# Sample keys turned by VectorE in blocks, latent queries in four column groups, expansions moved between the samples

## The chip, the cores and the metric

The kernel runs on one core of a Trainium2 chip. The metric is the device time of one execution in microseconds. The kernel before took 1524.16 us (median of 3 runs, 1523.92 to 1525.11).

## What is computed

One inference step of a two-layer trunk for a prompt of 512 tokens and for 8 samples of one token each. Layer 0 is a gated token MLP and a ConvFFN, layer 1 latent attention and a ConvFFN; everything is float32. The change touches the attention of layer 1 alone. There each sample attends over 2048 cached positions plus its own new one. A cached position has a latent of 256 numbers (`ckv`) and a rotary key of 64 (`kr`); both are shared by the 8 heads:

```python
s = (einsum('nthc,nsc->nhts', ql, ckv) + einsum('nthr,nsr->nhts', qp, kr)) * ATTN_SCALE
p = softmax(where(k_pos <= pq, s, -inf))
out = einsum('nhts,nsc->nthc', p, ckv)        # then o = out @ w_uv per head, and @ w_o
```

The query side `ql` is the head's query times `w_uk`. The prompt attends causally over its own 512 latents. The cache is paged: sample n's rows are gathered by a page table.

## The kernel before, in words

All activations lie transposed: features on the 128 partitions, 520 columns (512 prompt tokens, 8 samples). Each engine has its program written out by hand, in a fixed order, and the engines meet at semaphores. The weights of the dense layers stream through `ws`, are split into a high and a low part (`split`, L1559), and are multiplied in three products (L602).

The changed part stands between the query projections (L913) and prompt attention (L1107). In order:

- GpSimd gathers a sample's keys (L560 to L572): 128 partitions, each with 16 consecutive cache rows, as `lat` [16, 256] and `lar` [16, 64]. Three buffers (`RING`); the gather of sample g waits from g = 3 on for the weighted sum of sample g - 3 (`pv_done`).
- `turn(s, f)` (L945) transposes the keys on TensorE, ten fills of four 128x128 blocks each, into four PSUM banks. ScalarE and VectorE copy the fills into `kt` in turn (`turned_block`, L1447 and L1871).
- L998 to L1016: latent queries of the samples (`ukt` x `qn`), a pick of the rotary queries, copies into `qz` (per chunk 32 columns, of which 8 heads are used), and the samples' scores over their own new row.
- `score(s)` (L966): 12 matmuls of 512 columns with 32-column weights, four column groups, each holding one quarter of the positions.
- VectorE takes the maximum of each row of the scores (L1907) and its negative (L1909); ScalarE takes the exponentials (L1460); `turn_exps` (L978) transposes them in four 128x128 blocks, VectorE copies them (L1918), `weigh` (L985) makes the weighted sum of the latents (16 matmuls of 256 columns), ScalarE copies it out (L1468).
- The loop L1018 runs sample s's scores, then the transposes of sample s + 1 around `turn_exps(s)`, then `weigh(s)`.
- After the loop `expand(g)` (L1035) makes the prompt's keys and values: 16 expansions of two matmuls with 512 columns. Between them stand the small matmuls that merge the four quarters and the own row of each sample (L1057, L1062, L1063, L1071, L1080), with a chain of small VectorE operations (L1930 to L1990). Then `new_rows` (L1084) transposes the new cache rows, which ScalarE copies (L1488) and GpSimd writes out (L573). Prompt attention starts when `os_ready`, `n_ready` and the last copies are there (L1102).
- SyncE loads the weights `w_o` once all scores are done (L478), since `kt` lies over `ws`.

Of the kernel before, what the change touches and what calls it, by code (L numbers as in the profile page):

```python
# [39 lines left out]
FILLS = 10  # L40
# [35 lines left out]
CONST_COLS = K_SUB + 2  # L76
# [30 lines left out]
def constants():  # L107
# [21 lines left out]
    c[:, K_SELT:K_SELT + P] = p[:, None] == p[None, :] % 32  # L129
# [41 lines left out]
def trunk(nc, a, outs):  # L171
    ctx = ExitStack()
    with ctx:
# [13 lines left out]
        def plan(base, *items):  # L187
# [30 lines left out]
        selt = cst[0:H, K_SELT:K_SELT + P]  # L218

# [36 lines left out]
            ("osb", [NS, CL], F32), ("cksn", [320], F32), ("small", [16], F32), ("ml", [2 * NS], F32), ("st4", [GRP, 2 * NS], F32),  # L256
            ("gst", [GRP, 2, NS], F32), ("wd", [GRP + 1, NS], F32), ("wdl", [GRP, NS], F32), ("lsum", [3, NS], F32),
# [5 lines left out]
        kt, qz, kt_end = plan(ws_base, ("kt", [FILLS, 512], F32), ("qz", [4, NS, 32], F32))  # L263
        assert kt_end <= ws_base + 2 * size([STAGES, 1024])
        pe_, pts, pt_end = plan(tmp_base, ("pe_", [2, 512], F32), ("pts", [2, 512], F32))
# [4 lines left out]
        v, o, _ = plan(arena, ("v", [4, D], F32), ("o", [H, T], F32))  # L270
        ppt1, kn, ppt0, pr_end = plan(
            arena + size([4, D]) + size([H, T]), ("ppt1", [4, SEQ], F32), ("kn", [H, SEQ], F32), ("ppt0", [4, SEQ], F32))
        assert pr_end <= proj_end
        ppt = [ppt0, ppt1]
        pp, okn, ownp, olT, ok_end = plan(
            tmp_base, ("pp", [LAG, SEQ], F32), ("okn", [2, 320], F32), ("ownp", [KC, NS, H], F32), ("olT", [KC, H, NS], F32))
        assert ok_end <= arena
# [6 lines left out]
        def S(name):  # L284
# [35 lines left out]
        ukT_done, ukt_ready, ql_done, qsel_done, qz_clear, qz_ready, so_done, so_ready, sn_done, sn_ready, zpad = (S(n) for n in (  # L320
            "ukT_done", "ukt_ready", "ql_done", "qsel_done", "qz_clear", "qz_ready", "so_done", "so_ready", "sn_done", "sn_ready", "zpad"))
        kv_done, kv_read_a, kv_read_v, nT_done, n_ready, n_sent = (S(n) for n in (
            "kv_done", "kv_read_a", "kv_read_v", "nT_done", "n_ready", "n_sent"))
        cT_done, kt_a, kt_v, sc_done = (S(n) for n in ("cT_done", "kt_a", "kt_v", "sc_done"))
        mx_done, neg_ready, e_done, gat_done, merge, wd_exp, sct_done = (S(n) for n in (
            "mx_done", "neg_ready", "e_done", "gat_done", "merge", "wd_exp", "sct_done"))
# [32 lines left out]
        def st(k, g):  # L359

            return small[:, LAG * k + g % LAG:LAG * k + g % LAG + 1]

# [33 lines left out]
        def _(sp):  # L396
# [81 lines left out]
            sp.wait_ge(sc_done, NS)  # L478
# [114 lines left out]
        def _(pe):  # L593
# [351 lines left out]
            def turn(s, f):  # L945

                m = FILLS * s + f
                if f == 0:
                    pe.wait_ge(d_lat[s % RING], 32 * (s // RING + 1))
                if m < 4:  # L950
                    pe.wait_ge(ukt_ready, m + 1)
                elif m % 2:
                    pe.wait_ge(kt_v, (m - 4) // 2 + 1)
                else:
                    pe.wait_ge(kt_a, (m - 4) // 2 + 1)
                for i in range(4):
                    if f < 8:
                        j, c = f % GRP, f // GRP
                        src = lat[s % RING][:, 8 * (j // 2) + 2 * i + j % 2, c * P:(c + 1) * P]
                    else:  # L960
                        k = 8 * (f - 8) + 2 * i
                        src = lar[s % RING][:, k:k + 2, :].rearrange("p i c -> p (i c)")
                    mm = pe.transpose(psum[:, 4 + m % 4, i * P:(i + 1) * P], src, ident)  # L963
                mm.then_inc(cT_done, 1)

            def score(s):  # L966

                pe.wait_ge(kt_a, 5 * (s + 1))
                pe.wait_ge(kt_v, 5 * (s + 1))
                wait(pe, e_done, s - 1)  # L970
                for b in range(3):
                    for j in range(GRP):
                        q = qz[:, b if b < 2 else 2 + j % 2, s, :]
                        keys = kt[:, 4 * b + j, :] if b < 2 else kt[:, 8 + j // 2, :]
                        mm = pe.matmul(psum[32 * j:32 * j + 32, s % 2, :], q, keys, start=(b == 0), stop=(b == 2))  # L975
                mm.then_inc(sc_done, 1)

            def turn_exps(s):  # L978
                pe.wait_ge(e_done, s + 1)
                wait(pe, pts_ready, s)  # L980
                for i in range(4):
                    mm = pe.transpose(psum[:, 2, i * P:(i + 1) * P], pe_[:, s % 2, i * P:(i + 1) * P], ident)
                mm.then_inc(pT_done, 1)

            def weigh(s):  # L985
                pe.wait_ge(pts_ready, s + 1)
                wait(pe, osn_ready, s)
                for i in range(4):
                    for j in range(GRP):
                        mm = pe.matmul(psum[32 * j:32 * j + 32, 3, 0:CL], pts[:, s % 2, i * P + 32 * j:i * P + 32 * j + 32],  # L990
                                       lat[s % RING][:, 8 * (j // 2) + 2 * i + j % 2, :], start=(i == 0), stop=(i == 3))
# [61 lines left out]
            for g in range(4):  # L1053
                expand(g)
# [998 lines left out]
```

## Time and profile before

| | us |
|---|---|
| median of the runs | 1524.16 |
| the profiled execution | 1521.48 |
| its span, first to last instruction | 1519.2 |
| TensorE matmuls busy | 1466.4 (97%) |
| VectorE busy | 886.2 (58%) |
| ScalarE busy | 548.0 (36%) |
| GpSimd busy | 174.3 (11%) |
| mean granted clock of TensorE | 0.976 |

Engines in the profile: PE is TensorE's matmuls, PEld its weight loads, DVE VectorE, ACT ScalarE, POOL GpSimd, SP SyncE. A row of the chain of work that ended last gives start, length and what; a row of the lines gives line, engine, operation, output <- input, shapes, count, busy time, mean of one in ns and the idle time before it. The granted clock is a share of 2.4 GHz.

### The profile page before, as it was taken

Reading aid. Unit: us, or ns where it says so; the run is one execution under the profiler, and the core shown is the slowest. Engines: PE = TensorE matmul, PEld = TensorE weight load, DVE = VectorE, ACT = ScalarE, POOL = GpSimd, SP = SyncE. Lnnn points to the kernel's source line nnn. Section 1 sums busy time; section 2 is a strip of 40 time slices with the busy share of each in tenths; the row PEclk is TensorE's granted clock in tenths of the full one; section 3 lists DMA queues with packets and bytes.
Section 4 is the critical chain, followed back from the end, with each engine's and each line's share of the span. In section 5 each row is a group of like instructions: output and inputs, shape, how many; then the busy total and the mean of one; then the engine's idle time right before and its main releaser. Section 6 shows DMA issues by size and latency. Waiting matters only on the chain.

```text
span 1519.2 us, 29832 instructions
## 1 busy us (share of the span) xinstructions
PE 1466.4 (97%) x11437; PEld 1364.1 (90%) x11437; DVE 886.2 (58%) x1529; ACT 548.0 (36%) x874; POOL 174.3 (11%) x329
## 2 busy tenths in 40 slices
PE   6999999999999999999999999999999999999998
PEld 6999998998999999999899764545989999999997
DVE  4444664237888888433655453266378888885334
ACT  4444443245222222333651332234362222223334
POOL 1000000000222223100001010100002223221000
PEclk9999999999999999999999999689999999999999
DMA  8232222331333232333423372100213332322321
GB/s 238 85 85 69 83 69 72 97 96 40 95 89 97 83 97 72 91 92 90 148 70 153 139 278 57 46 1 1 84 46 103 88 97 83 97 77 85 97 86 65
DMA packets 224367, 138.14 MB, mean 91 GB/s; under 512 B 12620, under 2 KB 220674, under 8 KB 223256
## 3 DMA queue, kind: packets, MB, share of 16 engines
q1 hardware_dynamic: 219688, 112.37, 25.5%
q0 software_dynamic: 4224, 24.62, 4.3%
q8 instruction: 50, 0.82, 0.2%
q10 hardware_dynamic: 384, 0.16, 0.1%
q14 instruction: 21, 0.17, 0.0%
HBM read 133.82 MB, written 3.67 MB: 91 GB/s over the span
## 4 chain that ended last, share of the span: by engine, by line
PE 90%; DVE 4%; issue 1%; ACT 1%; DMA 0%; DVEq 0%; ACTq 0%
PE psum L602 73%; PE psum L963 2%; PE psum L1050 2%; PE psum L1115 2%; PE psum L975 2%; PE psum L1114 1%; PE psum L1132 1%; PE psum L990 1%; PE psum L658 1%; PE psum L757 1%; PE psum L1124 1%; DVE wl L1563 1%; DVE ut L1602 1%; DVE x L1605 1%; ACT wh L1185 0%
## 5 line engine op out<-in xcount | busy, mean ns | idle before, releaser
L1563 DVE TENSOR_TENSOR wl<-ws,wh 128x1024 fp32r<-128x1024 f32 x217 | 265.6, 1225 | 339.6 <-ACT wh L1188 173.9
L602 PE MATMUL psum<-xh,wh 128*128 128x260 f32 x2064 | 426.4, 286 | 13.6 <-DVE xl L1582 4.4
L602 PE MATMUL psum<-xh,wl 128*128 128x260 f32 x2064 | 420.6, 284 | 0.0
L602 PE MATMUL psum<-xl,wh 128*128 128x260 f32 x2064 | 420.1, 283 | 0.0
L602 PEld LDWEIGHTS psum<-xh,wh 128*128 128x128 f32 x2064 | 321.5, 189 | 17.0 <-issue 14.0
L602 PEld LDWEIGHTS psum<-xh,wl 128*128 128x128 f32 x2064 | 320.8, 189 | 0.0
L602 PEld LDWEIGHTS psum<-xl,wh 128*128 128x128 f32 x2064 | 320.3, 189 | 0.4
L1188 ACT ACTIVATE wh<-ws 128x1024 fp32r<-128x1024 f32 x144 | 152.1, 1056 | 319.5 <-PE psum L602 319.5
L602 PE MATMUL psum<-acth,wh 128*128 128x260 f32 x704 | 144.3, 284 | 0.0
L602 PE MATMUL psum<-acth,wl 128*128 128x260 f32 x704 | 143.2, 282 | 0.0
L602 PE MATMUL psum<-actl,wh 128*128 128x260 f32 x704 | 142.9, 282 | 0.0
L1185 ACT ACTIVATE wh<-ws 128x1024 fp32r<-128x1024 f32 x73 | 77.1, 1057 | 161.4 <-PE psum L602 161.4
L602 PEld LDWEIGHTS psum<-actl,wh 128*128 128x128 f32 x704 | 109.3, 188 | 0.1
L602 PEld LDWEIGHTS psum<-acth,wh 128*128 128x128 f32 x704 | 109.0, 188 | 0.3
L602 PEld LDWEIGHTS psum<-acth,wl 128*128 128x128 f32 x704 | 109.0, 188 | 0.0
L1383 ACT ACTIVATE cc<-cc 128x536 f32<-128x536 f32 x44 | 28.7, 652 | 161.9 <-DVE cc L1776 161.9
L520 POOL COPY cs<-ab 128x2 f32 (+1 forms) x88 | 40.0, 455 | 360.9 <-DVE ab L1759 360.9
L1773 DVE SCALAR_TENSOR_TENSOR cc<-ab,pt,cc 128x536 f32<-128x536 f32 x88 | 68.3, 777 | 12.2 <-DVE cc L1771 6.1
L1776 DVE SCALAR_TENSOR_TENSOR cc<-ab,pt,cc 128x536 f32<-128x536 f32 x88 | 68.4, 777 | 12.1 <-DVE cc L1773 4.7
L1757 DVE TENSOR_TENSOR ab<-psum,r 128x260 f32<-128x260 f32 x88 | 37.7, 428 | 37.6 <-PE psum L602 27.1
L517 POOL COPY ab<-pt 128x16 f32 (+1 forms) x88 | 56.7, 644 | 4.7 <-issue 4.7
L602 PE MATMUL psum<-ush,wh 128*128 128x260 f32 x256 | 53.3, 284 | 3.5 <-DVE wl L1563 3.5
(271 smaller groups left out, 1907.5 us busy)
## 6 DMA issues: line engine op xcount, KB each, us to landing
ws<-in_w_up SPq DMA_DIRECT2D x88, 512.0 KB, 3.8
ws<-in_w_in_a SPq DMA_DIRECT2D x32, 512.0 KB, 4.0
ws<-in_w_down SPq DMA_DIRECT2D x32, 384.0 KB, 3.1
ws<-in_w_down SPq DMA_DIRECT2D x32, 320.0 KB, 2.9
ws<-in_w_out_a SPq DMA_DIRECT2D x16, 512.0 KB, 3.6
ws<-in_w_o SPq DMA_DIRECT2D x8, 512.0 KB, 4.2
xn<-in_x_prompt SPq DMA_DIRECT2D x4, 512.0 KB, 10.3
ws<-in_w_dq SPq DMA_DIRECT2D x4, 512.0 KB, 4.1
```

Source lines behind the costliest of these rows:

```text
L517: pool.tensor_copy(dst[:, :, 0:2], st[:, :, :, bass.ds(f, 1)].rearrange("p s k o -> p s (k o)")).then_inc(state_in, 1)
L520: pool.tensor_copy(cs[:, 0:2, bass.ds(f, 1)].rearrange("p k o -> p (k o)"), ab[:, u % 2, SEQ:SEQ + 2])
L602: mm = pe.matmul(psum[:, 2 * slot + b, 0:HB], w, r[:, k, b * HB:(b + 1) * HB], start=st, stop=en)
L963: mm = pe.transpose(psum[:, 4 + m % 4, i * P:(i + 1) * P], src, ident)
L975: mm = pe.matmul(psum[32 * j:32 * j + 32, s % 2, :], q, keys, start=(b == 0), stop=(b == 2))
L1050: mm = pe.matmul(psum[:, bank, :], lw, r, start=(c == 0), stop=(c == KC - 1))
L1185: act.activation(weights(n)[0], ws[:, slot4, :], ACT.Copy).then_inc(w_high, 1)
L1188: act.activation(wh[:, slot2, :], ws[:, slot4, :], ACT.Copy).then_inc(w_high, 1)
L1563: dve.tensor_tensor(low_, ws[:, slot4, :], f32(high), ALU.subtract).then_inc(w_low, 1)
L1757: dve.tensor_tensor(ab[:, b, 2:2 + HB], a_b[:, 0, 0:HB], r1[:, 0:HB], ALU.mult)
L1773: dve.scalar_tensor_tensor(out=cc[:, b, :], in0=ab[:, b, 1:1 + CW_], scalar=w[1], in1=cc[:, b, :], op0=ALU.mult, op1=ALU.add)\
L1776: dve.scalar_tensor_tensor(out=cc[:, b, :], in0=ab[:, b, 2:2 + CW_], scalar=w[2], in1=cc[:, b, :], op0=ALU.mult, op1=ALU.add)\
```

## The change

Constants: `FILLS` becomes `CHUNKS = 5` with `QB = 10`, three small selection matrices are added. What it does:

- The keys are no longer transposed by TensorE. VectorE transposes each 32x32 block of a [128, 1024] chunk by itself (5 a sample) from `lat` / `lar` straight into `kt`. A block stays on its 32 partitions, so partition quarter i holds the keys of other positions than quarter j, and the queries are laid out block-diagonally: `qz` [10, 8, 32] has for quarter i only columns 8i to 8i + 7 filled. One column of the scores then is 4 positions by 8 heads in 32 rows.
- The scores of a sample are 5 chunks x 2 x 4 matmuls of 128 columns, in four column groups, with negative scale, so that minima stand for maxima. The minimum is shared by the positions of one head in a column group, by a transpose, a reduce and a transpose of 32 columns.
- The exponentials are turned by 16 ordinary matmuls of 32 columns against a spread identity.
- Twelve expansions stand before and between the samples, all copied by ScalarE; 12 and 13 stand in the merge, 14 and 15 behind the samples' outputs. The new rows stand ahead of these.
- `kn`, `v`, `okn` and others lie elsewhere; `ScalarE` clears half of `qz` and makes half of its copies.

The diff, cut to its core:

```diff
 TensorE
-            for f in range(FILLS):
-                turn(0, f)
+            def score(s, c):
+                n = CHUNKS * s + c
+                pe.wait_ge(kt_ready, n + 1)
+                if c == 0:
+                    wait(pe, e_done, s - 1)
+                for e in range(2):
+                    for g in range(GRP):
+                        mm = pe.matmul(psum[32 * g:32 * g + 32, s % 2, 0:P], qz[:, 2 * c + e, s, :], kt[:, c, e, g * P:(g + 1) * P],
+                                       start=(c == 0 and e == 0), stop=(c == CHUNKS - 1 and e == 1))
+                mm.then_inc(ch_done, 1)
             def turn_exps(s):
                 pe.wait_ge(e_done, s + 1)
                 wait(pe, pts_ready, s)
-                for i in range(4):
-                    mm = pe.transpose(psum[:, 2, i * P:(i + 1) * P], pe_[:, s % 2, i * P:(i + 1) * P], ident)
+                for m in range(4):
+                    for i in range(4):
+                        mm = pe.matmul(psum[32 * i:32 * i + 32, 2, 32 * m:32 * m + 32], pe_[:, s % 2, 32 * m:32 * m + 32],
+                                       spread[:, :, H * i:H * (i + 1)], start=True, stop=True)
                 mm.then_inc(pT_done, 1)
...
+            for e in range(2):
+                for r in range(2):
+                    for i in range(4):
+                        mm = pe.matmul(psum[32 * i:32 * i + 32, 1, (2 * r + e) * 32:(2 * r + e + 1) * 32],
+                                       ident[:, e * ROPE + 32 * r:e * ROPE + 32 * r + 32], qr[:, :, SEQ:T], start=True, stop=True)
             mm.then_inc(qsel_done, 1)
+            for g in range(2):
+                expand(g)
...
+            for c in range(CHUNKS):
+                score(0, c)
+            pe.wait_ge(so_ready, 2)
+            pe.transpose(psum[0:H, 3, 0:NS], so[0:NS, :], ident[0:NS, 0:NS]).then_inc(sn_done, 1)
+            pe.wait_ge(sn_ready, 1)
             for s in range(NS):
-                score(s)
...
                 if s + 1 < NS:
-                    for f in range(6):
-                        turn(s + 1, f)
+                    score(s + 1, 0)
+                expand(s + 2 if s < 6 else 2 * s - 4)
                 turn_exps(s)
                 if s + 1 < NS:
-                    for f in range(6, FILLS):
-                        turn(s + 1, f)
+                    score(s + 1, 1)
                 weigh(s)
+                if s >= 6:
+                    expand(2 * s - 3)
+                if s + 1 < NS:
+                    for c in range(2, CHUNKS):
+                        score(s + 1, c)
...
+            for c in range(5):
+                new_rows(c)
             pe.wait_ge(olT_ready, 1)
...
             mm.then_inc(os_done, 1)
+            for g in range(14, 16):
+                expand(g)
 ScalarE
+                act.activation(pe_[:, s % 2, :], psum[:, s % 2, 0:P], ACT.Exp, bias=mxe[:, s, 0:1], scale=-1.0,
+                               accum_out=ml[:, s:s + 1]).then_inc(e_done, 1)
...
+            for g in range(2):
+                expanded(g)
             for s in range(NS):
...
                 exps(s)
+                expanded(s + 2 if s < 6 else 2 * s - 4)
+                turned_exps(s)
+                outputs(s)
+                if s >= 6:
+                    expanded(2 * s - 3)
 VectorE
+            def turn_keys(s, c):
+                if c == 0:
+                    dve.wait_ge(d_lat[s % RING], 32 * (s // RING + 1))
+                wait(dve, ch_done, CHUNKS * (s - 1) + c + 1)
+                src = lat[s % RING][:, :, 64 * c:64 * c + 64] if c < 4 else lar[s % RING][:, :, :]
+                dve.transpose(kt[:, c, :, :].rearrange("p e (m b) -> p m e b", b=32),
+                              src.rearrange("p m (e a) -> p m e a", a=32)).then_inc(kt_ready, 1)
...
             for s in range(NS):
+                if s + 1 < NS:
+                    turn_keys(s + 1, 0)
+                dve.wait_ge(ch_done, CHUNKS * (s + 1))
...
+                dve.tensor_reduce(mxa[:, 0:1], psum[:, s % 2, 0:P], AX_X, ALU.min).then_inc(mx_done, 1)
                 dve.wait_ge(mx_done, s + 1)
+                dve.transpose(mxb[:, :], mxa[:, :]).then_inc(mx_step, 1)
+                dve.wait_ge(mx_step, 2 * s + 2)
+                dve.tensor_reduce(mxc[:, :], mxb[:, :].rearrange("p (i h) -> p h i", h=H), AX_X, ALU.min).then_inc(mx_step, 1)
+                dve.wait_ge(mx_step, 2 * s + 3)
+                dve.transpose(mxe[:, s, :].rearrange("p (i h) -> p i h", h=H),
+                              mxc[:, :].rearrange("p (o h) -> p o h", o=1).to_broadcast([P, 4, H])).then_inc(neg_ready, 1)
...
                 if s + 1 < NS:
+                    for c in range(1, CHUNKS):
+                        turn_keys(s + 1, c)
...
+            expanded(14)
             split(U_O, U_O % STAGES, U_O % 2)
             split(U_O + 1, (U_O + 1) % STAGES, (U_O + 1) % 2)
```

## Rows read from the trace of the kernel before

**Rows 1.** Page, chain that ended last: share of the span by engine.
```profile
PE 90%; DVE 4%; issue 1%; ACT 1%; DMA 0%; DVEq 0%; ACTq 0%
```

**Rows 2.** Windows: start:end, length, busy us (xcount), granted clock, DMA share, GB/s.
```profile
857.68:923.58 65.90, 65.82 (x700) 45.52 (x700) 33.48 (x55) 25.78 (x55) 9.43 (x10) 1.00 0.53 201
841.08:857.68 16.60, 14.70 (x113) 10.74 (x111) 7.13 (x18) 2.99 (x5) 1.89 (x2) 0.79 0.41 158
923.58:974.74 51.16, 45.51 (x186) 24.46 (x186) 12.63 (x33) 10.32 (x20) 3.45 (x7) 0.88 0.25 68
```

**Rows 3.** Chain in time (start, length, what), one sample's step.
```profile
864.57 2.58 PE psum L975 x24
867.15 2.77 PE psum L963 x24
869.92 0.44 PE psum L982 x4
870.36 1.75 PE psum L963 x16
872.10 1.86 PE psum L990 x32
```

**Rows 4.** Chain in time, from the last sample to prompt attention.
```profile
928.69 7.06 PE psum L1050 x16
...
952.39 3.84 PE psum L1071 x32
956.23 8.26 PE psum L1050 x12
964.49 3.47 PE psum L1080 x32
...
971.61 3.12 issue
```

**Rows 5.** Windows, granted clock of TensorE around the tail.
```profile
956.00:958.00 2.00, 2.00 (x5) 0.97 (x5) 0.00 (x0) 0.00 (x0) 0.00 (x0) 0.50 0.00 0
...
962.00:964.00 2.00, 2.00 (x6) 0.86 (x5) 1.00 (x3) 0.00 (x0) 0.00 (x0) 0.96 0.00 0
...
974.00:978.00 4.00, 3.27 (x8) 2.00 (x8) 0.74 (x3) 1.09 (x4) 2.13 (x4) 0.50 0.26 83
...
994.00:998.00 4.00, 4.00 (x9) 1.50 (x8) 1.62 (x6) 1.16 (x3) 0.00 (x0) 0.71 0.00 0
```

**Rows 6.** VectorE lines by form, 841 to 975: count, busy us, mean ns, idle.
```profile
L1878 DVE COPY kt<-psum 128x512 f32<-128x512 f32 x40 | 27.5, 690 | 6.3 <-PE psum L963 5.5
L1907 DVE TENSOR_REDUCE ml<-psum 128x1 f32<-128x512 f32 x8 | 5.5, 692 | 31.0 <-PE psum L975 31.0
...
L1563 DVE TENSOR_TENSOR wl<-ws,wh 128x1024 fp32r<-128x1024 f32 x2 | 2.4, 1222 | 2.3 <-ACT wh L1185 2.3
```

**Rows 7.** Chain in time: latent queries and rope pick before sample 0.
```profile
846.06 3.47 PE psum L1001 x32
849.53 0.59 PE psum L1007 x8
```

**Rows 8.** Timeline: four weight loads of the next score round.
```profile
864.82 0.13 PEld L975 LDWEIGHTS psum<-kt,qz 128*32 128x32 f32 x4 [0.30 <-issue]
```

**Rows 9.** Lines by form: small VectorE operations, 841 to 975.
```profile
L1970 DVE TENSOR_REDUCE wpr<-wp 128x8 f32<-128x32 f32 x1 | 0.2, 206 | 0.0
```

**Rows 10.** Lines by form, prompt attention: 128-column VectorE reduce.
```profile
L2000 DVE TENSOR_REDUCE small<-psum 128x1 f32<-128x128 f32 x8 | 2.3, 292 | 0.3
```

**Rows 11.** Lines by form, prompt attention: 128-column ScalarE exponential.
```profile
L1526 ACT ACTIVATE pp<-psum,small 128x128 f32<-128x128 f32 x8 | 2.9, 368 | 5.7 <-DVE small L2004 5.7
```

**Rows 12.** Timeline, GpSimd: the gather of sample 3 and its issue.
```profile
864.88 0.94 POOL L571 DMA_INDIRECT lat<-in_cache_ckv,idx  x1 [21.16 <-PE psum L990]
866.12 0.94 POOL L572 DMA_INDIRECT lar<-in_cache_kr,idx  x1 [0.30 <-issue]
```

**Rows 13.** DMA issues, 830 to 935: count, median us to landing.
```profile
lar<-in_cache_kr,idx POOLq DMA_INDIRECT x6, 8.0
```

More of the change, by code:

```diff
@@ L39 @@
 RING = 3
-FILLS = 10
+CHUNKS = 5
+QB = 10
 LAG = 3
@@ L1053, in _ @@
-            for g in range(4):
-                expand(g)
-            pe.wait_ge(merge, 1)
-            pe.matmul(psum[0:H, 0, 0:2 * GRP * NS], selh, st4[:, :, :].rearrange("p a b -> p (a b)"), start=True, stop=True).then_inc(gat_done, 1)
-            for g in range(4, 9):
-                expand(g)
-            pe.wait_ge(merge, 11)
+                if s >= 6:
[3 more added lines that the diff above has]
+                        score(s + 1, c)
@@ L1062, in _ @@
+            pe.wait_ge(merge, 2)
+            pe.matmul(psum[0:H, 0, 0:32], selh, st4[:, :, 0:NS], start=True, stop=True)
+            pe.matmul(psum[0:H, 0, 32:64], sel8, st4[:, :, NS:2 * NS], start=True, stop=True).then_inc(gat_done, 1)
+            expand(12)
+            pe.wait_ge(merge, 12)
             pe.matmul(psum[:, 0, 64:96], selt, wd[0:H, 0:GRP, :].rearrange("p a b -> p (a b)"), start=True, stop=True)
             pe.matmul(psum[:, 0, 96:160], ones[0:H, :], wdg[0:H, :, :].rearrange("p a b -> p (a b)"), start=True, stop=True).then_inc(sct_done, 1)
-            for g in range(9, 13):
-                expand(g)
@@ L1067, in _ @@
-            pe.wait_ge(merge, 15)
+            expand(13)
+            pe.wait_ge(merge, 16)
             pe.wait_ge(osn_ready, NS)
@@ L1073, in _ @@
             mm.then_inc(olp_done, 1)
-            for g in range(13, 16):
-                expand(g)
-            pe.wait_ge(olT_ready, 1)
-            for h in range(H):
-                for c in range(KC):
-                    mm = pe.matmul(psum[:, 0, h * NS:(h + 1) * NS], uv[:, c, h * P:(h + 1) * P], olT[:, c, h, :],
-                                   start=(c == 0), stop=(c == KC - 1))
-            mm.then_inc(os_done, 1)
             def new_rows(c):
@@ L1098, in _ @@
                 new_rows(c)
+            pe.wait_ge(olT_ready, 1)
+            for h in range(H):
+                for c in range(KC):
+                    mm = pe.matmul(psum[:, 0, h * NS:(h + 1) * NS], uv[:, c, h * P:(h + 1) * P], olT[:, c, h, :],
+                                   start=(c == 0), stop=(c == KC - 1))
+            mm.then_inc(os_done, 1)
+            for g in range(14, 16):
+                expand(g)
             pe.wait_ge(os_ready, 1)
             pe.wait_ge(n_ready, 5)
-            pe.wait_ge(kv_read_v, 8)
-            pe.wait_ge(kv_read_a, 8)
             def scores(g):
@@ L1508, in _ @@
                 new_rows(c)
+            expanded(15)
             def turned(g):
@@ L1899, in _ @@
+            mm.then_inc(qown_ready, 1)
+            for i in range(2):
+                for r in range(2):
+                    mm = dve.tensor_scalar(rope_rows(i, r), psum[32 * i:32 * i + 32, 1, r * 64:(r + 1) * 64].rearrange("p (e h s) -> p s h e", e=2, s=NS),
+                                           -SCALE, None, ALU.mult)
+            mm.then_inc(qz_v, 1)
+            for c in range(3, CHUNKS):
+                turn_keys(0, c)
             dve.wait_ge(so_done, 1)
@@ L1977, in _ @@
             mm.then_inc(merge, 1)
-            for g in (12, 14):
-                expanded(g)
             dve.wait_ge(olp_done, 1)
-            dve.wait_ge(merge, 15)
+            dve.wait_ge(merge, 16)
             for c in range(KC):
```

308 lines of the change are left out of this document (137 added, 171 removed).

## The prediction

> **What bounds the kernel now.** I read the chain that ended last first: TensorE holds 90% of the span [rows 1], so a change pays where it shortens TensorE's own queue, or the waits in it. All edited code runs between about 841 us (end of the query projections) and 974.74 us (first score of prompt attention). I cut that stretch in three [rows 2]: before the first turned key of sample 1 (16.6 us), the sample loop up to the last score (65.9 us), and the end (51.2 us). In the loop TensorE is busy for 65.8 of 65.9 us at a granted clock of 1.00; VectorE has 33.5, ScalarE 25.8. So the loop is bound by TensorE's instructions, not by DMA (share 0.53). The chain in time then gives one sample's step [rows 3]: scores 2.58, 24 key transposes 2.77, transposes of the exponentials 0.44, 16 more key transposes 1.75, weighted sum 1.86: 9.40 us, of which 4.52 are the key transposes. The end [rows 4] is a queue too: 16 records of expansions in 7.06 us (an ordinary fp32 matmul shows as two records of weight load and matmul; an expansion is two such matmuls, 4 records, 1.77 us; all sixteen 28), 32 eight-column records in 3.84, and before prompt attention a wait of 3.12 us. Last, the granted clock [rows 5]: behind the sparse eight-column matmuls it is 0.50 of 2.4 GHz (1.2 GHz) and dense expansions bring it back in some 6 us (12 records take 8.26 instead of 7.06 x 12/16 = 5.3 us); behind the 3.12 us wait it is 0.50 again and comes back only around 996 us, so that the first 21 us of prompt attention run at the low level.
>
> **What is removed.** 40 key transposes a sample leave TensorE: 8 x 4.52 = 36 us. On VectorE 5 x 0.69 us of copies, the 0.69 us copy of the turned exponentials and the 0.69 us maximum go [rows 6].
>
> **What is added on TensorE, per sample.** Scores become 40 matmuls of 128 columns, in 10 rounds over four column groups, in place of 12 of 512. Streaming is 10 x 128 against 3 x 512 columns: 2.58 x 1280/1536 = 2.15 us is the floor. The ceiling is if the number of weight loads decides: the weighted sum makes 32 pairs of records in 1.86 us, 0.058 each [rows 3]; 80 pairs would be 4.65 us. Two rows speak for the floor: a full load of 128 columns and its matmul are 0.108 us a pair (3.47/32 [rows 7]), so 32 columns load in about 0.027; and four loads to different groups start within 0.13 us in all [rows 8]. I take the overhead of the weighted sum over its streaming (1.86 - 4 x 0.43 = 0.15 in 4 rounds, 0.04 each): 2.5 us. The transposes of the exponentials become 16 ordinary matmuls of 32 columns, 32 pairs: between 0.86 (0.027 each) and 1.86 (0.058); 1.0 taken, by the rows on loads. The weighted sum keeps its 16 matmuls, 1.86. One expansion of 1.77 comes in. Sum 2.5 + 1.0 + 1.86 + 1.77 = 7.1 us.
>
> The rows show nothing slower than 0.058 us a pair with narrow weights [rows 3, 7, 8]. The Trainium skill, TensorEngine Tiling (Array Packing), Instruction Overhead, speaks against cutting columns: each matmul costs some 60 cycles however few columns it has. By it alone the 80 records of a sample's scores would take 2.0 us, as an estimate from that page, under the streaming floor; counted for loads too it would be 4.0, and the sum would come out some 6 us worse. No row here shows 128 columns in four groups.
>
> **What is added on VectorE, per sample.** Five block transposes of 128x1024. The trace has no such operation. The nearest of that size is a subtraction at 1.22 us [rows 6], one element a cycle and lane; I take 1.2. Above, I bound it by reading and turning one after the other, 2.44; below, by half, 0.6, as if two elements went at once. The Trainium skill, Vector Engine (DVE) Microarchitecture Reference, section 3.8, says that the transposing front end sustains one element per cycle per lane; no run here shows that yet. The maxima become three operations on 32 columns or fewer at about 0.21 [rows 9] and a 128-column reduce 0.29 [rows 10], with hand-overs 1.0 us. Sum 5 x 1.2 + 1.0 = 7.0 us, beside TensorE's 7.1: just hidden. ScalarE: exponential of 128 columns 0.37 [rows 11], 0.2 allowed for its sum and the hand-over, and three copies out of PSUM: under 3 us even at VectorE's 0.69 each, hidden.
>
> **The wait that moves in: the gathers.** Sample s+3's keys are gathered once the weighted sum of s frees their buffer. The two gathers are issued 0.3 us after it and 1.24 us apart [rows 3, 12] and each lands 8.0 us after its issue [rows 13]: 0.3 + 1.24 + 8.0 = 9.55 us after the weighted sum. Before, the next need was 12.0 us away (2.58 + 6.82 + 2.58), so 2.4 us were spare. After, VectorE's wait on that gather stands at the head of step s+2, and queued behind it are the maxima of sample s+2, on which ScalarE's exponentials and TensorE's turn wait. The loop through two steps is 9.55 + block transpose 1.2 + first score chunk 0.5 + expansion 1.77 + turn 1.0 + chunk 0.5 + weighted sum 1.86 = 16.4 us: 8.2 us a sample. That, not 7.1, is the new bound.
>
> **Stretch by stretch.** *Start:* the 32 eight-column records (3.47) start at about 842, with the last query projection, instead of 846.1, as nothing is transposed ahead; the rope pick becomes 32 pairs (1.0 instead of 0.59); two expansions follow. As the clock fell behind those records before (0.79 mean [rows 2]) I charge both at half clock, 7.1 us, to 854. Own scores and sample 0's scores end at about 857; with the maxima TensorE resumes at 858.3 against 857.68: +0.6. VectorE's and ScalarE's 27 small copies of the queries (about 0.25 each) lie beside the expansions; uncovered they would cost 3 us. *Loop:* stepping the loop above from 858.3, with the first two steps at 7.1 to 7.2 and the rest at the gather's pace, the last weighted sum ends at 921.5 and expansion 11 at 923.3: 65.0 us, against 71.0 before (857.68 to 928.69), -6, and twelve of sixteen expansions are done. *End:* 0.2 + 1.77 + 1.0 (a merge chain of some 14 small operations at 0.2, 2.8 us, behind one expansion) + 0.58 + 1.77 + 3.84, then new rows (3.65 before) at the low clock 4.6, the eight-column product 3.47 [rows 4] at the low clock 6.9, two expansions at mostly low clock 6.6: 27.3 us, against 46.05 (974.74 - 928.69): -18.7. The wait of 3.12 us (the eviction of the new rows waits for its two buffers to be written out) is gone, as 13 us of other work now lie beside it. VectorE's two splits (2.4 us) now follow its last expansion copy and lie beside expansion 15 and the first scores; late next is nothing. *Prompt attention:* it starts behind 6 us of dense expansions rather than a wait. If the clock is back then, as after 962 [rows 5], 21 us at half speed become 10.5: I take -9.
>
> Sum: 0.6 - 6 - 18.7 - 9 = -33 us. The profiled execution took 1521.48 us (span 1519.2); 1488.4 for it. The median of the runs is 2.7 above: 1524.2 - 33 = **1491 us**.
>
> **The rivals.**
> (a) *The clock does not come back before prompt attention* (for: there it stayed at 0.50 for 21 us [rows 5]; against: dense expansions lifted it in 6): -24, **1500**.
> (b) *Weight loads and instruction floors decide narrow matmuls*: scores 4.65, turn 1.86, so 10.1 us a sample, over the gather's 8.2, + 16 us: **1507**. Against it: rows 7 and 8.
> (c) *The loop turns cold*: TensorE pauses about 2 us in every second step for a gather; if the clock falls there, half of the 5.6 us of work in each round trip is added over and over, about + 15 us: **1506**. Against: the matmuls between the pauses are dense ones in four groups, as those under which the loop's clock is 1.00 [rows 2].
> (d) *VectorE becomes the bound, slower than before*: at 2.44 us a block transpose it needs 13.2 us a sample, + 40 us: **1531**. It decides from 2.3 us a transpose (8 x 12.3 = 98 = 65 + 33).
> (e) *Nothing moves* because the expansions, put in the gather's shadow, lengthen it as much as they fill it: about **1524**. The spare TensorE time in [rows 2] after 36 us less work speaks against it.
>
> **How the numbers follow.** Forecast 0.50, (a) 0.17, (b) 0.12, (c) 0.07, (d) 0.12, (e) 0.02. A difference of 0.2%, 3 us, is about what a measurement of this kernel can tell from none. Faster: 0.50 + 0.17 + 0.12 + 0.07 = 0.86; same 0.02; slower 0.12. The range goes up to 1511, past (b), and down to 1480: scores at their floor (-3), the turn at its floor (-1), the clock not falling in the end (-7).
>
> **What would show it.** Block transposes of 1.1 to 1.25 us on VectorE; score chunks of 0.5 us; steps of 7.1 us first and 8.2 later, with TensorE idle until a gather lands; loop end near 923; the first prompt score near 951 at a clock of 1.00 soon after. Wrong if a transpose is over 2 us, if a chunk takes 0.9, or if a gather lands much later than 8 us because VectorE and GpSimd get in each other's way.

## The result, and the profile after

The changed kernel takes 1488.11 us (median of 4 runs, 1483.39 to 1489.3) against 1524.04 us for the kernel before (4 runs, 1522.46 to 1525.11): ratio 0.9759, 95% interval 0.9739 to 0.9779. It is faster, 3 us under the forecast of 1491 us. The profiled execution took 1483.39 us. First its page: shares of the span by engine, and the chain that ended last.

```profile
PE 1419.5 (96%) x11815; PEld 1331.4 (90%) x11815; DVE 898.8 (61%) x1542; ACT 533.9 (36%) x862; POOL 173.2 (12%) x329
PE 86%; DVE 6%; DMA 2%; issue 2%; ACT 1%; POOL 0%; DVEq 0%; ACTq 0%
```

TensorE's share of the chain went from 90% [rows 1] to 86%, and DMA, absent before, has 2%: the forecast wait for gathers. Next the windows of the changed kernel, stage by stage (columns as in [rows 2]): start, loop, end and prompt attention.

```profile
835.85:849.16 13.31, 12.23 (x160) 8.60 (x160) 12.92 (x31) 4.68 (x17) 1.21 (x2) 0.87 0.52 199
849.16:921.20 72.04, 59.79 (x1115) 33.54 (x1116) 45.28 (x64) 13.48 (x41) 9.44 (x10) 0.91 0.55 206
921.20:946.39 25.19, 24.50 (x105) 16.88 (x105) 6.54 (x23) 5.49 (x10) 5.41 (x10) 0.73 0.16 46
946.39:1022.27 75.88, 72.70 (x272) 37.43 (x272) 50.34 (x171) 35.01 (x105) 0.00 (x0) 1.00 0.05 15
```

And two windows of the kernel before, which answer to the second and the fourth of them: its loop as the prediction cut it, and prompt attention up to the first output matmul.

```profile
857.68:928.69 71.01, 68.41 (x737) 46.95 (x737) 35.14 (x58) 26.83 (x58) 9.43 (x10) 1.00 0.55 203
974.74:1060.69 85.95, 82.81 (x272) 41.52 (x273) 49.93 (x170) 34.41 (x104) 1.95 (x4) 0.87 0.01 4
```

| stretch | before | after | measured | forecast |
|---|---|---|---|---|
| start | 15.5 | 13.3 | -2.2 | +0.6 |
| loop | 71.0 | 72.0 | +1.0 | -6 |
| end | 46.05 | 25.2 | -20.9 | -18.7 |
| prompt attention | 85.95 | 75.9 | -10.1 | -9 |
| sum | 218.5 | 186.4 | -32.1 | -33 |

So the sum is right to 1 us, but the loop gained nothing where 6 us were forecast, and the other three made up for it. TensorE's busy time fell by 46.9 us in all (1466.4 to 1419.5); 11.8 us of that are lost again in three pauses of the loop (4.24, 4.32 and 3.22 us), in which it waits for gathered keys. The times differ by more than the sum: 35.9 us by the medians, 38.1 by the profiled executions. The changed stretch starts at 835.85 us in this trace and at 842.14 in that of before, on code that the diff does not touch; the run of the unaltered changed kernel, below, shows that this point wanders, and with what.

The loop's loss shows in the chain in time (start, length, what), here two steps of the changed kernel. L1903 is the block transpose, L979 scores, L990 the turned exponentials, L1001 the weighted sum, L1016 an expansion, L596 and L597 the two gathers.

```profile
854.81 0.95 POOL lat L596
...
856.06 9.12 DMA lar<-in_cache_kr,idx
...
865.20 1.26 DVE kt L1903
...
866.50 0.84 PE psum L979 x16
867.34 3.37 PE psum L1016 x4
870.71 0.39 PE psum L990 x32
871.10 0.48 PE psum L979 x16
871.58 1.96 PE psum L1001 x32
...
873.80 0.94 POOL lat L596
```

From gather to gather it is 873.80 - 854.81 = 19.0 us for two samples, where 16.4 were forecast. The chain has the forecast members in the forecast order. Two differ in size: the gather lands 9.12 us after its issue instead of 8.0 [rows 13], and the expansion takes 3.37 us instead of 1.77; on the other side the turn takes 0.39 instead of 1.0. Why 3.37: the timeline shows TensorE idle for 4.24 us ahead of the score chunk,

```profile
866.50 0.84 PE L979 MATMUL psum<-kt,qz 128*32 128x128 f32 x16 [4.24 <-DVE kt L1903]
```

and the windows behind the three pauses:

```profile
865.20:869.00 3.80, 2.50 (x18) 1.22 (x19) 3.69 (x7) 0.46 (x2) 0.00 (x0) 0.71 0.97 412
884.30:888.00 3.70, 2.42 (x18) 1.43 (x19) 3.60 (x7) 0.46 (x2) 0.00 (x0) 0.50 0.93 396
903.00:907.00 4.00, 2.77 (x18) 1.39 (x19) 3.90 (x7) 0.46 (x2) 0.00 (x0) 0.67 0.00 0
```

The granted clock behind the pauses is 0.71, 0.50 and 0.67 (0.50 is the 1.2 GHz level), where the loop of before ran at 1.00 throughout. DMA is at 0.93 to 0.97 of its engines behind the first two: the gathers of two samples are in flight together. Behind the third it is at 0.00, and the expansion there takes 3.19 us all the same. So it is the clock that stretches these expansions, not the traffic of the gathers.

### The profile page after: what moved, and what is told of

Its sections match the earlier page's. It is cut to its first block, busy times and chain, and to the rows that moved or that the text cites. A ratio compares the mean times of both kernels' runs of the same rounds, so it can differ in the third digit from the quotient of the medians.

```text
span 1480.6 us, 30514 instructions
## 1 busy us (share of the span) xinstructions
PE 1419.5 (96%) x11815; PEld 1331.4 (90%) x11815; DVE 898.8 (61%) x1542; ACT 533.9 (36%) x862; POOL 173.2 (12%) x329
## 4 chain that ended last, share of the span: by engine, by line
PE 86%; DVE 6%; DMA 2%; issue 2%; ACT 1%; POOL 0%; DVEq 0%; ACTq 0%
PE psum L627 74%; DMA lar<-in_cache_kr,idx 2%; PE psum L1016 2%; PE psum L1125 2%; PE psum L1145 1%; PE psum L1124 1%; DVE ut L1627 1%; DVE x L1630 1%; PE psum L782 1%; PE psum L1134 1%; DVE wl L1588 1%; DVE kt L1903 1%; PE psum L1001 1%; PE psum L683 1%; PE psum L1106 0%
```

## The experiments

The theory after the result: the loop is bound by the round trip of a gather, as forecast, and the 2.6 us that a pair of steps is over the forecast are an expansion that stands in that trip at half clock. The rivals are that VectorE sets the pace, or that bandwidth does. "The loop" below goes from the last small copy of the start (`sown`, 849.0 us in the changed kernel) to the first merge matmul (72.1 us in the changed kernel), "the region" from the first clearing of the query tile (`qz`) to the first split of prompt attention's output (217.8 us before, 185.5 after). That split starts 0.8 us ahead of the first output matmul, so prompt attention is given shorter by as much here than in the table above.

**The expansion ahead of the wait.** In each step the expansion is moved from behind the first score chunk to ahead of it.

```diff
+                expand(s + 2 if s < 6 else 2 * s - 4)
                 if s + 1 < NS:
                     score(s + 1, 0)
-                expand(s + 2 if s < 6 else 2 * s - 4)
```

> Only TensorE's order in the sample loop changes: expansion, then the first score chunk of the next sample. Theory G (the loop is paced by the round trip weighted sum, gather, first block transpose, maxima, weighted sum, and the pause in it cools TensorE): a late gather now has the expansion beside it, at full clock, instead of behind it at half clock (3.4 us). The pair of steps falls from 19.0 to about 16 us, the loop from 72 to about 63, the time from 1488 to about 1479. Rival V (VectorE's 7 us of work a sample is the pace): nothing moves, 1488.

Measured: 1481.01 us (median of 4 runs, 1480.54 to 1485.48), ratio to the kernel before 0.974 (0.9715 to 0.9765); loop 64.4 us. The loop gives back 7.7 us, near the 9 expected, and the rival that VectorE sets the pace, by which nothing would move, is out. Its window of the loop, and then a pair of steps:

```profile
853.80:918.20 64.40, 55.86 (x1113) 31.82 (x1114) 45.37 (x66) 13.56 (x41) 9.44 (x10) 1.00 0.64 230
```

And in the chain:

```profile
859.41 0.94 POOL lat L596
...
860.66 8.94 DMA lar<-in_cache_kr,idx
...
875.63 0.94 POOL lat L596
```

The pair is 16.2 us, the clock 1.00, TensorE's busy time 4 us less than in the changed kernel for the same matmuls. The gather still lands 8.9 us after its issue. So the expansion behind the pause was the loss, partly as work in the round trip and partly through the clock.

**No gathers in the loop.** The gathers of samples 3 to 7 and the waits on them are left out; the loop works on the first three samples' rows again, which leaves out part of the computation.

```diff
-            for g in range(NS):
+            for g in range(RING):
...
-                if c == 0:
+                if c == 0 and s < RING:
```

> Leaves out the gathers of samples 3 to 7; these samples use the keys of samples 0 to 4 that lie in the buffers, so their outputs are not the reference's. Theory G: with no gather to wait for, all steps take what the first two take, 6.5 us; the loop falls from 72 to about 53 us, the time to about 1469. Rival V: VectorE paces the loop at 7.0 us a sample, and it falls to 58 at best. If gathers cost nothing, 72 stays.

Measured: 1475.89 us in one run, loop 55.8 us, 16.3 us shorter. Its window of the loop:

```profile
858.40:914.30 55.90, 54.43 (x1116) 31.49 (x1116) 44.89 (x66) 13.49 (x42) 0.00 (x0) 1.00 0.12 31
```

TensorE is busy for 54.43 of 55.90 us at a clock of 1.00, VectorE for 44.89. A step with one expansion takes 6.7 us (the score chunks at 872.04 and 885.48 stand two samples apart), against 7.1 forecast for TensorE and 7.0 for VectorE. It is not TensorE alone that sets it: 6.7 of the 13.4 us of such a pair lie on VectorE in the chain, the maxima and five block transposes in 5.64 us. The loop lies between the 53 us of the theory and the 58 us of the rival, and the time is 7 us over the 1469 expected, with the region starting late, at 845.3 us. The distance to 72.1 is what the gathers cost, pauses and clock together.

**The maxima first.** VectorE finishes the maxima of sample s before the first block transpose of s+1, so nothing of sample s waits behind the gather of s+1.

```diff
-                if s + 1 < NS:
-                    turn_keys(s + 1, 0)
...
-                    for c in range(1, CHUNKS):
+                    for c in range(CHUNKS):
```

(and TensorE's first score chunk of s+1 moves behind the turn in the same way, so the expansion stands ahead of it here too, as in the first edit).

> VectorE takes the maxima of sample s before it turns the first chunk of sample s + 1, and TensorE turns the exponentials before the first score chunk. Theory G: a late gather then no longer holds up the maxima; the trip for two steps is gather 10.6 + block transpose 1.3 + chunk 0.5 + weighted sum 2.0 = 14.4, 7.2 a sample, and VectorE's row of maxima 1.0, five transposes 6.0 and the last chunk 0.5 make 7.5: loop about 60, time about 1476. Rival: the first block transpose no longer hides under the scores, and that costs what the gather gives back: loop 70 or more.

Measured: 1478.93 us (4 runs, 1478.24 to 1479.21), ratio 0.9718 (0.9699 to 0.9737); loop 63.4 us, 3 more than expected. One step of its chain shows what paces it now (L1901 is the block transpose):

```profile
871.12 5.76 DVE kt L1901 x5
...
876.93 0.64 PE psum L979 x14
...
877.85 0.39 PE psum L979 x2
...
878.27 0.30 DVE mxa L1944
...
879.22 5.72 DVE kt L1901 x5
```

Five block transposes, the last score chunk, the maxima, and again: 8.1 us with nothing of the gathers in it. That is as much as a step of the first edit takes (16.2 us a pair), where the gathers set the pace. The gain over the first edit is 1 us of loop. Its four runs lie below those of the first edit, by 2.1 us at the medians, but the intervals of the two ratios overlap.

**The rotary gather early.** The rotary rows' buffer is free once its keys are turned, so its gather goes ahead of the latent rows' one, with a semaphore of its own.

```diff
+                if g >= RING:
+                    pool.wait_ge(kt_ready, CHUNKS * (g - RING + 1))
+                    pool.indirect_dma_start(lar[g % RING]..., None, runs_r, at_row).then_inc(d_lar[g % RING], 16)
+                    pool.wait_ge(pv_done, g - RING + 1)
```

(VectorE then waits for the latent rows ahead of transpose 0 and for the rotary rows ahead of transpose 4.)

> The changed kernel, with the rotary keys of sample s + 3 gathered as soon as those of s have been turned, so that behind the weighted sum only the latent gather stands. Theory G: the trip loses 1.25 us of issue and some 1.2 us of transfer, the pair of steps falls from 19.0 to about 16.6, the loop from 72 to about 65. If what matters is only the order of VectorE's queue, 72 stays.

Measured: 1482.07 us in one run, loop 64.2 us, as expected, and as much as moving the expansion alone gave. Its window of the loop, where the clock is 1.00 again:

```profile
853.70:917.90 64.20, 57.41 (x1112) 31.71 (x1112) 45.22 (x66) 13.46 (x41) 8.52 (x9) 1.00 0.63 228
```

TensorE's busy time is 2.4 us less than in the changed kernel, and 3.9 less with the expansion ahead of the wait: that part of the 8 us is the clock. TensorE's pauses in the two loops are 1.7 us or less. With the maxima first as well:

> maxima_first, and the rotary keys of sample s + 3 are gathered as soon as those of s have been turned, with a semaphore of their own. Theory G with VectorE next: the gather has 2.4 us more of slack but no longer sets the pace, so within 2 us of maxima_first, about 1475. If the gather still sets it there, 5 us or more under maxima_first.

Measured: 1478.82 us (4 runs), ratio 0.972 (0.9694 to 0.9745), loop 60.7 us: the same time as with the maxima first, as expected (though 4 us over the 1475 named). VectorE paces both. The loop is 2.7 us shorter, but the regions differ by 0.6 us only (176.0 and 176.6). In the chain above the last score chunk is broken by a halt of 0.29 us for which the trace names no releaser; here it is not. Then with the expansion moved instead:

> The changed kernel with two edits together: each sample's expansion is made right behind its weighted sum, ahead of the next pair's wait, and the rotary rows' gather is issued ahead of the latent rows' gather. My theory is that a pair of steps in the changed kernel (19.0 us) is set by the round trip of a gather, and that the expansion at half clock (3.4 us) and the late rotary gather (about 1.2 us a step) stand in that trip. Alone the first edit gave a loop of 64.4 us and the pair still waited for its gathers. If both terms add, the loop falls to 58 to 61 us, the changed region to 172 to 176 us and the time to 1473 to 1478 us, at or under the 1478.9 us of the kernel that keeps the maxima first. The rival is that the gathers are bound by what the DMA rings move (about 6.5 us a sample): then an earlier rotary gather only shares the same bandwidth, the loop stays at 64 us and the time at 1481 us, as with the first edit alone.

Measured: 1476.89 us (5 runs, 1475.58 to 1481.74), ratio 0.9702 (0.9675 to 0.9729); loop 61.4 us, region 176.2: the time as expected, loop and region just over their ranges. It is the lowest median of the study, but the intervals of the ratios overlap with those of the two kernels above, so that no difference among the three is shown. The pair of steps in its chain (L1005 is the weighted sum, L1909 the block transpose):

```profile
861.74 8.54 DMA lat<-in_cache_ckv,idx
...
870.30 1.25 DVE kt L1909
...
874.28 1.77 PE psum L1005 x32
...
876.31 9.43 DMA lat<-in_cache_ckv,idx
```

876.31 - 861.74 = 14.6 us for the first pair, down from 19.0 and 16.2, and 15.5 for the second (19.75 and 16.5 in the other two kernels). The rotary term gives 1.6 and 1.0 of the 2.4 us expected of it. What is left is the latent gather itself, 8.5 to 9.4 us of each pair. The bandwidth rival (no better than 64 us) falls, by 3 us of loop and no more.

**The expansions back behind the loop.** The ten expansions of the loop are put behind it, in one row.

```diff
-                expand(s + 2 if s < 6 else 2 * s - 4)
...
+            for g in range(2, 12):
+                expand(g)
```

> The changed kernel with expansions 2 to 11 behind the sample loop. If they lie free in the gather's shadow, the loop stays at 72 and the time rises by ten expansions, 17.7 us, to 1506. If, as the trace says, each that stands behind a late gather is on the path at half clock (3.4 us), the pair of steps falls to about 16, the loop to about 62, and the time is about 1497.

Measured: 1498.13 us (4 runs, 1494.55 to 1500.26), ratio 0.9821 (0.9804 to 0.9837); region 192.5 us, 7.0 more. The second branch of the expectation (1497 us) holds. The loop to its last weighted sum falls to 61.8 us, then comes this row of the chain:

```profile
920.25 17.36 PE psum L1016 x40
```

Ten expansions cost 17.4 us behind the loop; inside it they had cost the difference, about 10 us. The pauses hide some 7 us of them. In the steps at the gather's pace the forecast had one expansion of each two in the round trip, at 1.77 us, and the other hidden: less than that half is hidden, and the one in the trip runs at the low clock.

**The new rows last, and the order of the end alone.** In the changed kernel the new rows' transposes and their evictions come ahead of the eight-column product and the last two expansions. The first edit puts it last again; the second does the reverse in the kernel before.

```diff
-            for c in range(5):
-                new_rows(c)
+            for g in range(14, 16):
+                expand(g)
...
+            for c in range(5):
+                new_rows(c)
```

> The changed kernel with the end in the old order: expansions 14 and 15 ahead of the samples' outputs, the new rows last. If the wait for the write-outs (3 us) and the low clock behind it are what prompt attention got rid of, both come back: +3 us of wait, +10 in prompt attention, -2 in the end itself, about 1499. If prompt attention gained from something else (where keys and values lie), only +3: 1491.

> The kernel before with the new order of the end alone (new rows, samples' outputs, expansions 14 and 15). Same theory from the other side: the 3.1 us wait goes, prompt attention starts at full clock, -10, and the sparse run in the end costs some 5 us at half clock: about 1516. If the clock does not come back, 1524 or above.

Measured: 1493.41 us (4 runs, 1488.52 to 1499.99), ratio 0.9812 (0.9785 to 0.9838) for the first. The profiled execution is the fastest of the four, 1488.52 us. Two rows of its chain, and the window of its first prompt scores:

```profile
930.82 3.47 PE psum L1106 x32
...
937.10 3.57 DMA out_new_kr_prompt<-okn
```

and the window:

```profile
941.70:962.00 20.30, 20.30 (x39) 9.16 (x40) 8.84 (x33) 4.66 (x16) 1.92 (x4) 0.50 0.05 17
```

The wait of [rows 4] is back (3.57 us for the rows to be written out) and prompt attention's first 20.3 us run at 0.50 as in [rows 5]: prompt attention takes 85.2 us instead of 75.2, the +10 expected. The end itself is 1.8 us shorter, as the eight-column product, now behind dense expansions, takes 3.47 us (first row above) and not 6.92. The loop, too, is shorter, 68.3 us on code that took 72.1 and 72.5 elsewhere. So the region is 4.5 us longer, and the medians differ by 5 and not by the 11 expected; whether the loop was shorter in the three slower executions, no trace shows. The timeline says where: here sample 4's latent gather is issued 8.0 us after sample 3's, and in the changed kernel's first trace 6.45 us. First the kernel with the new rows last:

```profile
855.90 0.95 POOL L596 DMA_INDIRECT lat<-in_cache_ckv,idx  x1 [17.44 <-PE psum L1001]
863.90 0.95 POOL L596 DMA_INDIRECT lat<-in_cache_ckv,idx  x1 [5.80 <-PE psum L1001]
886.23 0.65 PE L979 MATMUL psum<-kt,qz 128*32 128x128 f32 x16 [2.88 <-DVE kt L1903]
```

And the changed kernel:

```profile
854.81 0.95 POOL L596 DMA_INDIRECT lat<-in_cache_ckv,idx  x1 [17.44 <-PE psum L1001]
861.26 0.95 POOL L596 DMA_INDIRECT lat<-in_cache_ckv,idx  x1 [4.26 <-PE psum L1001]
885.58 1.08 PE L979 MATMUL psum<-kt,qz 128*32 128x128 f32 x16 [4.32 <-DVE kt L1903]
```

Two gathers that start close together arrive close together, so one step in two gets a long pause (3.2 to 4.3 us) and then a slow expansion; spread more evenly, the pauses are 1 to 2.9 us, and only one of the four expansions behind them was slow (867.60, 3.48 us). That one stood behind a pause of 2.00 us, and the one behind the pause of 2.88 us was not slow, so the length of the pause does not settle it alone. What spread the gathers was a halt of some 1.5 us among the scores of samples 1 and 2, in pieces for which the trace names no releaser; its cause is open.

The second took 1509.84 us (4 runs, 1508.92 to 1511.35), ratio 0.9908 (0.9892 to 0.9925): prompt attention 77.0 us, 8.2 less, with the granted clock at 1.00 in its first 20 us, the end 1.3 longer. The region is 212.4 us, 5.4 less than before, so of the 32 us of the change the order of the end alone is worth 5 to 8, without any of the new transposes. The time fell by more, 14 us by the medians, where 8 were expected; 6.5 us of that lie ahead of the region (start at 835.6 us against 842.1), on code that the edit does not touch.

**Each block transpose twice.**

```diff
+                dve.transpose(kt[:, c, :, :]..., src...).then_inc(turned_once, 1)
+                dve.wait_ge(turned_once, CHUNKS * s + c + 1)
                 dve.transpose(kt[:, c, :, :]..., src...)
```

> The changed kernel with each block transpose on VectorE done twice, the second over the first, so that a block of 128x1024 costs 2.42 us and not 1.21 us. This is the condition of the prediction's rival in which VectorE becomes the bound of the loop (2.44 us a transpose, 1531 us against the forecast 1491 us, with the break-even against the kernel before at 2.3 us). If the rival's sum holds, a sample's step is 5 x 2.42 us plus about 1 us of maxima, 13.1 to 13.4 us, the loop rises from 72 to 105 to 110 us and the time from 1488 to 1521 to 1528 us. The other possibility is that the gather pauses of the changed kernel take part of it up: its pair of steps is 19.0 us, of which VectorE works some 13 us, so a pair would rise to 26.4 us only if no pause is left, and the loop to about 106 us; if a pause of 2 us a pair is left beside it, the loop is 114 us and the time 1531 us.

Measured: 1519.49 us in one run, region 217.1 us, loop 94.7 us. Its window of the loop, then the block transposes in it (twice 1.2 us a block),

```profile
860.80:955.50 94.70, 71.54 (x1113) 36.48 (x1114) 86.87 (x100) 13.83 (x41) 9.44 (x10) 0.80 0.43 157
```

and by line and form:

```profile
L1907 DVE STREAM_TRANSPOSE kt<-lat 128x1024 f32<-128x1024 f32 x27 | 33.6, 1246 | 0.9
L1904 DVE STREAM_TRANSPOSE kt<-lat 128x1024 f32<-128x1024 f32 x27 | 32.5, 1203 | 0.0
```

VectorE, at 86.87 of 94.70 us, is the bound, a step is 12.9 us, no wait for a gather is left in the chain, and the region is within a microsecond or so of the 217.8 us of the kernel before: rival (d) had its mechanism right, and its break-even lies just over 2.45 us a transpose (forecast 2.3). The 105 to 110 us expected of the loop were over 10 too high: they count eight steps, and sample 0's transposes lie ahead of the loop, so that seven of 12.9 us are in it. Its time, 1531 us, was 11.5 too high: start and loop took 20.8 + 94.7 = 115.5 us where it had 15.5 + 0.6 + 8 x 13.2 = 121.7, as a step is 12.9 us and sample 0's transposes lie under the start's other work in part, and the stretches ahead of and behind the loop were better than forecast.

**The changed kernel again,** unaltered.

> The changed kernel with nothing altered. In the traces so far the point at which the latent queries' stage starts lies anywhere between 835.6 and 845.3 us although the code ahead of it is the same in all, so one profile's total says less than the stretch from that point to the first output matmul. My theory: that stretch is again 185 to 187 us (before: 217.8 to 218.5 us), the start lies anywhere between 835 and 846 us, and the median of the timed runs is 1485 to 1491 us, so that the change is worth 32 to 36 us. The rival, that the change also shortens the work ahead of that point, would put the start below 838 us again and the median at 1485 us or lower.

Measured: 1489.55 us (5 runs, 1487.16 to 1493.31), ratio 0.978 (0.9753 to 0.9808). The region is 185.9 us, its start at 845.2 us, and the profiled execution took 1493.11 us, 9.7 more than the first one. The theory holds: what the change touches repeats to half a microsecond, and the point where it starts lies between 835.6 and 845.4 us over the traces of this study. Two executions of identical code differ there by 9.4 us. In the region the change is worth 32 us; the medians, 35.9 and 33.7 us less than before, have that scatter in them.

Most of the wandering is the granted clock in the code ahead. In the two traces of this kernel, 3.0 of the 9.4 us are there by an early wait of 2.04 us on TensorE (it ends at 42.81 and at 45.81 us), for a reason that was not looked for. The other 6.4 open up behind waits that both executions have, where the clock fell in one and not in the other. The largest such stretch, first in the first trace, then in this one:

```profile
740.00:750.00 10.00, 9.48 (x67) 8.70 (x66) 9.58 (x18) 7.15 (x15) 0.00 (x0) 1.00 0.44 159
740.00:750.00 10.00, 7.13 (x29) 5.96 (x28) 7.96 (x16) 7.10 (x17) 1.48 (x2) 0.66 0.86 307
```

In both the same wait of 2.36 us stands just ahead of the same matmuls (it ends at 738.57 and at 744.30 us). So part of what the first measurement shows beyond 32 us is an execution whose clock held upstream.

## Why the prediction came out right, and which steps of it did not

That the total is off by 3 us only is partly luck. The loop was worth 7 us less than forecast, and the start, the end and prompt attention together 6.1 us more (2.8, 2.2 and 1.1), each for a reason of its own. The measured time also has the early start of the region in it.

**Block transposes.** 1.2 us taken between 0.6 and 2.44. By form, VectorE in the loop of the changed kernel (busy, mean ns, idle and its releaser):

```profile
L1903 DVE STREAM_TRANSPOSE kt<-lat 128x1024 f32<-128x1024 f32 x27 | 31.6, 1210 | 10.9 <-DMA lar<-in_cache_kr,idx 10.7
L1948 DVE TENSOR_REDUCE mxa<-psum 128x1 f32<-128x128 f32 x7 | 1.9, 275 | 10.0 <-PE psum L979 10.0
```

1.21 us: right, by the row nearest in size. The Trainium skill (Vector Engine (DVE) Microarchitecture Reference, section 3.8) gives its transposing front end a rate of one element per cycle and lane. This number agrees with it: a block takes as long as the subtraction of 1.22 us, and not half or twice as long. Transposes and maxima of a sample come to 7.0 us as summed.

**Narrow matmuls.** Rival (b) is false. Sample 0's scores stand alone in the start of the changed kernel, in the timeline:

```profile
839.98 5.14 PE L1016 MATMUL psum<-ckt,uk 128*128 128x512 f32 x8
845.58 2.39 PE L979 MATMUL psum<-kt,qz 128*32 128x128 f32 x80
870.64 0.46 PE L990 MATMUL psum<-cst,pe__135 128*32 128x32 f32 x32
```

80 records in 2.39 us: 2.5 was taken, the streaming floor was 2.15. The turn of the exponentials was mis-sized, 1.0 taken, 0.39 to 0.46 measured, under the lower bound of 0.86: that bound charged each of 32 narrow loads 0.027 us in a row, and a pair of load and matmul took 0.012 us. That the four column groups overlap would explain it and fits [rows 8], but no run here tests it alone. The Trainium skill's 60 cycles for each matmul (TensorEngine Tiling (Array Packing), Instruction Overhead) would be 0.025 us at 2.4 GHz, as an estimate from that page. Counted for each record, as the prediction did, the turn disagrees with it (32 records, 0.012 us each). Counted for each matmul of the program, of which fp32 makes two records, it agrees (16 matmuls, 0.024 us each).

**The start.** +0.6 forecast, -2.2 measured. The term that failed is the clock behind the eight-column records: both expansions were charged at the low level, 7.1 us, and took 5.14 (above), 2.0 of the 2.8 us. The rope pick, 32 narrow records like the turn, took 0.63 instead of 1.0.

**The loop.** -6 forecast, +1.0 measured: here the prediction was wrong by 7 us. The round trip was named rightly, with its members. It put the gather at 8.0 us, read from a loop that issues one sample's gathers every 9.4 us. In the new loop two samples' gathers are issued 6.45 us apart (854.81 and 861.26) and share the DMA, and the one that ends each trip lands 9.1 to 9.2 us after its issue: 1.1 us a pair. The last gather, issued 13.3 us after the one ahead of it, lands in 8.10. And it put the expansion behind the pause at 1.77 us; at the low clock it takes 3.4 to 3.7: 1.6 to 1.9 a pair. The turn gives 0.6 back. That is 2.1 to 2.4 of the 2.6 us a pair, and the first score chunk, 0.84 us instead of 0.5, is most of the rest. It is a matter of spacing too: the forecast stepped the loop as if the gathers came every 8.2 us, and they came 6.45 and 12.5 us apart. Rival (c), "the loop turns cold", said that this would happen if the clock fell in the pauses, and it was ruled unlikely because dense matmuls lie between them. They do, but the pauses are 4.24, 4.32 and 3.22 us and not the 2 us that it assumed: two of three gathers are later, and TensorE's own work in a step is shorter (6.7 us without gathers, 7.1 forecast). Its +15 us was too high, since only the work right behind each of three pauses is slow. Moving that expansion gave 7.7 us back.

**The end and prompt attention.** The product behind the new rows took 6.92 us for 6.9 forecast, the last two expansions 6.11 for 6.6, as in the chain of the changed kernel:

```profile
926.59 3.47 PE psum L1082 x32
...
933.36 6.92 PE psum L1106 x32
940.28 6.11 PE psum L1016 x8
946.39 0.22 PE psum L1124 x2
```

The rest of the 2.2 us by which the end was better: new rows 3.3 instead of 4.6, and 3.47 instead of 3.84 for the eight-column records of L1082. Rival (a), that the clock would not be back, is false: 1.00 from 946.39 on. Putting the new rows last brings the low clock back (0.50 for 20.3 us) and costs the 10 us, so this reading was put to the test and held.

**Nothing moves** (e) is false by 32 us, though its reason, expansions that lengthen the gathers' shadow, is what took 7 us from the loop.

## What to carry to other kernels

Where a loop becomes bound by the round trip of a buffer, let only work that the next transfer needs stand between the arrival of the data and the freeing of the buffer; filler goes ahead of the wait. Here that one move was worth 7.7 us of a loop of 72. Read the landing time of a transfer from the trace only with the spacing that the new loop will have. Before a large rewrite, look at what stands just ahead of a long stretch of matmuls: a wait there cost 10 us of prompt attention, and a different order alone gave 8 of them back. And compare two kernels by the stretch that the change touches: here the code ahead of it moved by up to 10 us between executions.

## What the runs showed of the hardware beyond the forecast

- Four column groups of 32 take 32-column fp32 matmuls at 0.012 us a record (32 in 0.39) and 128-column ones at 0.030 (80 in 2.39); a matmul of the program makes two such records.
- In the changed kernel's first trace, pauses of 3.2 to 4.3 us on TensorE inside dense work were followed by a granted clock of 0.50 to 0.71 for about one expansion; where the loop's pauses were shorter, it was mostly 1.00, with one slow expansion behind a pause of 2.00 us and none behind one of 2.88 us.
- Gathers of two samples issued 6.45 us apart moved about 400 GB/s together (windows of 3.7 and 3.8 us), and the first of them landed 9.1 to 9.2 us after issue; 9.4 us apart they took 8.0, and the last one, alone, 8.1.
- The same upstream code ended up to 10 us apart from execution to execution (835.6 to 845.4 us); behind the same wait of 2.36 us the granted clock of a window of 10 us was 1.00 in one and 0.66 in the other.
